# Holding back scatters of routing records at four points of a hybrid S5 and mixture-of-experts step

## What is computed

```python
x = x + ssm_mixer(rmsnorm(x, norm_mix))      # S5 scan, Re(C x) + D u, GELU, then a @ w_out with a gate
x = x + hier_moe(rmsnorm(x, norm_ffn))       # below
y = rmsnorm(x, norm_final)

def hier_moe(x):                             # per token
    g = argmax(softmax(x @ w_rg))            # top 1 of 4 groups
    w1, w2, e1, e2 = top_k(softmax((x @ w_re)[g]), 2)   # top 2 of the 4 experts in it, weights normalised
    return sum over e in (e1, e2) of  p_g * w_e * (silu(x @ w_gate[e]) * (x @ w_up[e])) @ w_down[e]
```

## Time and profile before

| | us |
|---|---|
| median of 3 runs | 830.38 (829.59 to 834.03) |
| profiled execution, own time | 831.41 |
| its span on the core | 829.7 |
| TensorE busy (matmul) | 785.4, 95% |
| VectorE busy | 598.2, 72% |
| ScalarE busy | 412.2, 50% |
| GpSimd busy | 316.4, 38% |
| record scatters L549 | 34 of 1.05 us mean, 324.6 to 436.9 |

### The profile page before, as it was taken

One profiled execution on the slowest core, in us unless ns is written; L12 is line 12 of the kernel. 1 busy time (PEld: TensorE's weight loads), 2 busy tenths in 40 slices (PEclk: granted clock), 3 DMA queues, 4 the chain that ended last, 5 costly groups with the idle time before them and its releaser, 6 DMA issues.

```text
span 829.7 us, 15186 instructions
## 1 busy us (share of the span) xinstructions
PE 785.4 (95%) x4265; PEld 619.3 (75%) x4265; DVE 598.2 (72%) x1143; ACT 412.2 (50%) x770; POOL 316.4 (38%) x416
## 2 busy tenths in 40 slices
PE   6999989999999999998988989999999999999993
PEld 4888866556778778786766868888888888887772
DVE  7998789996534365457776788768687688687843
ACT  7566752225335353342353666647466477466622
POOL 3910011011000002304154566567566766565532
PEclk9999999999999999999999999999999999999997
DMA  8564316897734242323367587557775688786632
GB/s 296 166 224 181 127 29 206 209 156 210 296 118 151 77 153 102 128 108 124 102 230 283 191 304 256 194 190 264 270 252 198 216 287 295 253 301 203 224 116 85
DMA packets 57670, 161.27 MB, mean 194 GB/s; under 512 B 21856, under 2 KB 26464, under 8 KB 50912
## 3 DMA queue, kind: packets, MB, share of 16 engines
q1 hardware_dynamic: 34304, 112.99, 41.6%
q0 software_dynamic: 22976, 47.05, 16.2%
q10 hardware_dynamic: 288, 0.03, 0.0%
HBM read 129.07 MB, written 62.40 MB: 231 GB/s over the span
## 4 chain that ended last, share of the span: by engine, by line
PE 38%; DMA 3%; issue 3%; DVE 2%; POOL 2%; DVEq 1%; ACTq 1%; ACT 1%; POOLq 0%
PE pbig L1391 7%; PE pbig L1395 7%; PE pbig L1392 7%; PE pbig L1410 4%; PE pbig L1412 4%; PE pbig L1411 4%; PE pbig L1327 3%; POOL records L549 1%; DMA xg<-x_mid,recs 1%; PE pbig L1403 1%; DMA WR<-in_w_gu 1%; DMA records<-rec,at_rec 1%; DVE WL L2014 1%; ACT WH L928 1%; DMA low<-records 0%
## 5 line engine op out<-in xcount | busy, mean ns | idle before, releaser
L1391 PE MATMUL pbig<-WH,xgH 128*128 (+1 forms) x304 | 123.9, 408 | 1.2 <-issue 1.1
L1392 PE MATMUL pbig<-WL,xgH 128*128 (+1 forms) x304 | 119.8, 394 | 0.0
L549 POOL DMA_INDIRECT records<-rec,at_rec x34 | 35.6, 1047 | 190.7 <-DVEq L2007 181.3
L1274 PE MATMUL pbig<-w2H,ysH 128*128 128x512 f32 x256 | 105.3, 411 | 0.0
L1275 PE MATMUL pbig<-w2L,ysH 128*128 128x512 f32 x256 | 100.6, 393 | 0.0
L1276 PE MATMUL pbig<-w2H,ysL 128*128 128x512 f32 x256 | 100.5, 393 | 0.0
L2014 DVE SCALAR_TENSOR_TENSOR WL<-WR,gf_p,WH 128x512 f32 (+1 forms) x128 | 86.2, 746 | 0.0
L928 ACT ACTIVATE WH<-WR,gf_p 128x512 f32 (+1 forms) x128 | 80.6, 712 | 3.6 <-DMA WR<-in_w_gu 1.5
L1395 PE MATMUL pbig<-WH,xgL 128*128 (+1 forms) x304 | 77.0, 395 | 0.0
L623 POOL DMA_INDIRECT x_sums<-xg,recs x36 | 61.7, 1713 | 35.7 <-DVE xg L2118 21.8
L946 ACT ACTIVATE sl<-pbig,recs 128x256 f32<-128x256 f32 x40 | 18.9, 473 | 102.8 <-PE pbig L1395 92.8
(11 more groups left out here) (356 smaller groups left out, 1738.3 us busy)
## 6 DMA issues: line engine op xcount, KB each, us to landing
WR<-in_w_gu SPq DMA_DIRECT2D x32, 1024.0 KB
WR<-in_w_dn SPq DMA_DIRECT2D x16, 1024.0 KB
xT<-in_x_cols SPq DMA_DIRECT2D x16, 512.0 KB, 3.7
low<-in_x_rows SPq DMA_DIRECT2D x16, 512.0 KB, 4.6
U<-in_x_rows SPq DMA_DIRECT2D x16, 512.0 KB, 5.1
x_mid<-x SPq DMA_DIRECT2D x16, 512.0 KB, 2.7
x_sums<-x SPq DMA_DIRECT2D x16, 512.0 KB, 4.0
w<-in_w_out SPq DMA_DIRECT2D x1, 4096.0 KB, 13.8
```

What stands on the lines that cost most here:

```text
L1274: pe.matmul(pbig[:, n, :], ysH[b][:, k, :], w2H[n][:, k, :], start=(k == 0), stop=False)
L1391: pe.matmul(pbig[:, 6, :], xgH[b][:, k, :], WH[:, ds(off + k * 2 * DE, 2 * DE)], start=(k == 0), stop=False)
L1392: pe.matmul(pbig[:, 6, :], xgH[b][:, k, :], WL[:, ds(low_ + k * 2 * DE, 2 * DE)], start=False, stop=False)
```

## The change

GpSimd waits at four points inside `file_rows` for a count of `lt_evac`, the semaphore that ScalarE increments when it has copied a tile's logits. The count 11 stands for tile 10, 12 for tile 11, 15 for tile 14, and TT = 17 for tile 16. Each wait stands ahead of one scatter, given by (tile, c). The waits divide the 34 scatters: 4, 4 and 4 of batch 0; 5 and 5 of batch 1; 4 and 4 of batch 2; batch 3 (4) is as before.

```diff
 BATCHES = ((0, 6), (6, 11), (11, 15), (15, TT))
+HOLD = {(2, 0): 11, (4, 0): 12, (8, 1): 15, (13, 0): TT}
 ROUTE_A, POS_AT, ROUTE_B = (7, 11, 15), (8, 12), (9, 13)
...
                 for c in range(2):
+                    if (t, c) in HOLD:
+
+                        pool.wait_ge(S["lt_evac"], HOLD[t, c])
                     pool.indirect_dma_start(tabD, bass.IndirectOffsetOnAxis(ap=at_rec[0:rows, c, t:t + 1], axis=0),
```

## The result

The changed kernel takes 824.38 us (median of 20 runs, 823.09 to 829.53), and the kernel before, run in turn with it, 832.04 us (20 runs, 827.24 to 834.79). The ratio is 0.9924, 95% interval 0.9909 to 0.9939: faster by 0.76%, some 6.3 us, where 4.6 us were forecast (the two medians alone lie 7.66 us apart). The profiled execution takes 825.51 us with a span of 823.8 us, against 831.41 and 829.7 us.

A forecast was written before the change was run, and what follows sets the result against it. TensorE was taken to bound the kernel, losing time to late handshakes beside scatter runs; 1.45, 3.65 and 5.08 us accumulated, limited to 4.6 by gather(3)'s landing: 830.38 - 4.6 = 825.8 us, 8-in-10 range 824.1 to 830.7.

The forecast's parts named there:

- What bounds the stage, and the mechanism: Routing to fourth expert slot: TensorE bounds at 12.94 us per tile; long scatter runs delay signals, above all TensorE to ScalarE.
- three late handshakes: Late ScalarE copies at tiles 10, 14 and 16, inside scatter bursts; losses of 1.45, 3.52 and 1.43 us.
- VectorE as next late: Before tile 15's mixing: first expert's weight cuts limit the gain to 3.65 us, not 4.97; 1.32 us lost.
- Batch 2's hold: Fifth scatter waits for tile 16's copy: costs 0 to 0.2 us; copy 1.43 us less late, 5.08 us gained on TensorE.
- A copy is late beside a group of four: Sign of being wrong: a copy still late although its scatter run is cut to four.
- the records land with the weight loads: Batch 2's last records land when the weight loads drain, 3.65 us earlier, even if the hold costs a microsecond.
- Gather(3): Rows for the fourth expert slot: issued 3.65 us earlier at 438.4, landing 4.6 us earlier at 447.4, where TensorE resumes.
- my rule: Gather(3)'s landing follows the end of the second expert's first loads, not its own issue; 4.6 us earlier, bounds 3.65 and 5.08.
- Gather(0): Behind batch 1's scatters: issued at about 397.1 instead of 394.75, rows wanted at 407.8; covered, barely in the worst case.
- (A): Rival: signals come in time, but gather(3) lands 9.96 us after issue; 826.7 us, variant 828.2; chance 0.20 with variant.
- (B): Rival: something else delays signals, or four or five scatters suffice; delays stay or move; 830.4 us, chance 0.14.
- (C): Rival: holds add to stalls that stay, delaying gather(3) by 1.6 us; 832.0 us, 832.5 with gather(0); chance 0.09.

The follow-up runs named there:

- chip 14: Unedited changed kernel timed again beside the kernel before, on another chip and occasion: 826.03 us against 830.12, ratio 0.9947 (0.9922 to 0.9972).
- split8: Changed kernel with other splits: batch 0 as 8 and 4, batch 1 as 8 and 2, batch 2 as 2 and 6; 827.19 us, one run.
- chip 3: Unedited changed kernel timed a third time beside the kernel before, on another chip: 826.24 us against 825.52, ratio 1.001 (0.9996 to 1.0023).
- hold_batch0: Kernel before plus only the two waits in batch 0: 825.07 us beside 826.35, ratio 0.9987 (0.9965 to 1.001).
- chip 0: Where the kernel before was timed beside itself and beside each batch's hold alone: 826.35 us (35 runs); itself again 827.23, ratio 1.001 (0.999 to 1.003).
- burst22: Changed kernel with its holds replaced by one: batches 0 and 1 in one run of 22 scatters after tile 13's copy; 841.11 us, one run.
- late12: Changed kernel with batch 0's twelve scatters all held until tile 10's logits are copied, other holds unchanged; 830.45 us, one run.

## Why the prediction was right, and where its steps were not

**What bounds the stage, and the mechanism.** Right where the two were first timed. The three late handshakes were the loss, the holds remove the first two entirely, and each gain is there: tile 11's logit matmuls moved by 351.15 - 350.74 - 1.86 = -1.45 us (forecast 1.45), tile 14's by 391.00 - 394.03 - 1.86 = -4.89 us (4.97).

**VectorE as next late.** Right. The mixing of tile 15 starts in the same moment as the weight cut ends, without an idle gap, and moved by 3.72 us (3.65); that of tile 16 by 3.60 us (3.65). Without this step the sum would have had 1.3 us more than the stage could give (4.89 less 3.60).

**Batch 2's hold.** Two sizes were off. Tile 16's copy comes 1.39 us after its matmuls (418.15 - 416.76), so 0.68 of the 1.43 us stayed, with only four scatters ahead of it; chip 14 shows the same, 0.69 us. "A copy is late beside a group of four" was one of the three signs by which I would be wrong, and it came, at less than half the size. The fifth scatter then comes at 419.19. Without the hold it would have come at 419.66 - 3.60 + 1.86 = 417.92, so the hold costs 1.27 us and not 0 to 0.2. Of this, 0.68 is the late copy. The other 0.59 is a price that I had put at nothing: from the end of the awaited copy to the held scatter pass 0.76 us here (418.43 to 419.19), and 0.75 and 0.76 at the two holds of batch 0 (copies end at 339.21 and 352.15), but only 0.28 at batch 1's (391.99 to 392.27). The three stand ahead of a tile's first scatter, the cheap one ahead of its second; the other traces with these holds give the same within 0.02 us. On PE the gain was 4.38 us (ready at 447.93 against 450.45) and not 5.08. That the records land with the weight loads, which was to hide such a delay, held only in part: the loads moved by 3.60 us (415.15 against 416.89), the table load behind the landing by 2.85 us (427.69 against 428.68). It cannot hide the whole 1.27 us.

**Gather(3).** It was issued 2.67 us earlier (forecast 3.65), and the second expert's loads 3.57 us earlier (forecast 4.6). By my rule, landing with the loads, PE's start on its rows should have moved by 3.57 us at most. It moved by 5.72. The first half of the rule holds: the gather's first packets came at 446.93 before and at 445.22 now, moved by 3.57 us, exactly as the loads. In all thirteen traces that show it they come 7.1 to 7.5 us after the issue of the loads. They also come 4.0 to 4.2 us after the gather's own issue in twelve of them (4.9 in the kernel before), so the traces favour the loads, but not by much.

My evidence for the rule was weaker than I took it to be. The 99.9% for the other queue in 443 to 444 says nothing, because a gather moves nothing so soon: gather(2), issued at 430.80 with the engines idle, has its first packet at 432.4, 1.6 us later, and gather(0), issued at 394.75, at 397.05, 2.3 us later. Nor do the engines work for the loads alone until these have drained. In 445 to 446 the kernel before kept them busy for 66.8% with the loads, and the gather still moved nothing. Once its packets were there, in 447 to 448, the two queues took nearly equal numbers of packets (q0 carries the gathers, q1 the loads; packets, MB, share of the 16 engines' time):

```profile
q1 hardware_dynamic: 37, 0.28, 66.5%
q0 software_dynamic: 33, 0.14, 33.7%
```

In the changed kernel the loads fill 444 to 445, and the gathers have 446 to 447 almost to themselves:

```profile
q1 hardware_dynamic: 52, 0.43, 102.6%
```

```profile
q0 software_dynamic: 87, 0.35, 97.2%
q1 hardware_dynamic: 8, 0.02, 6.1%
```

The Trainium skill (DMA: Bandwidth & Descriptors, section Queues, rings and completion order) states an even turn, packet by packet. The 37 and 33 packets agree with that; what held the gather back until 446.93 they do not tell.

What I had taken as fixed was the time from the first packet to the landing. Before, PE waited until 452.04, 5.1 us after it; now it could start 3.0 us after it. Before, gather(4) and gather(5) had been issued (443.71 and 445.16) when service began, now only gather(4) (442.69; the next is at 445.52). That the fewer waiting gathers made the difference is an argument from these times and was not tried. Most other traces fit it (2.8 to 3.1 us where PE waits for the rows), but split8 took 4.2 us with only one gather waiting behind.

**Gather(0).** Wrong, without a cost. I had it at about 397.1, and it was issued at 403.81, 7.2 us later than before (9.06 less 1.86). It waits for the first table load, and I took this to wait for batch 0 alone. It waits for batches 0 and 1: FIRST_TOK is BATCHES[1][1] = 11. In the same way `tab_early` counts the tiles below 15, not below 11. Both are wrong in the description of the kernel ahead of the prediction. SyncE issues that load only at 401.83, 1.2 us after batch 1's last scatter, and its store of tile 15 waits behind it. The profile had shown this: before, the load was issued behind the end of batch 1 (391.58).

```profile
392.74 0.38 SPq L450 DMA_DIRECT2D low<-records  x1
```

Batch 1 also ended later than I had it, since its scatter at 393.63 took 3.22 us, beside VectorE's weight cut (393.73, 2.28 us); whether the cut is the cause was not tried. PE took up the rows at 409.55, so 5.7 us were enough.

**The size.** Forecast 4.6 us of gain and 825.8 us, measured 6.3 us by the ratio and 824.38 us. The stage of the trace gives 5.7: two terms fell short together by 0.7 us on PE, and gather(3)'s landing more than made up for it. That the total came out near the forecast is therefore in part luck. The rest lies between executions. The base of three runs (830.38) was 1.7 us below the median of twenty, and the delays of the kernel before differ from one execution to the next.

**The rivals.** (A) did not come: PE started on gather(3)'s rows 7.0 us after its issue, not 9.96. (B), that something else makes the signals late, is half true: the run of scatters is needed, and so is something outside the program. It also named a move of the delay to another handshake, and a small one came, at tile 15 (below). On the chips without it the outcome is the one that (B) gives, no change. (C) did not come, but its mechanism, a held scatter that delays gather(3), may stand behind PE's wait of 1.12 us on chip 3 and of 2.14 us in split8. It is not shown: hold_batch0, where batch 2 is not held, has such a wait of 0.76 us too, and the kernel before on chip 0 has none.

**Open.** What makes the handshakes late in one place and not in another, and whether it belongs to the chip or to the occasion. The scatters are issued at the same pace in both (1.27 us apart), so the issue times hold no hint. Open also is from which length of run on it matters, and how the gain of the first comparison divides among the holds except as the trace's terms divide it.

## What to carry to other kernels

A wait that nothing on the core explains, beside a run of work on another engine, is worth a cheap pause in that run, placed where the waiting engine has just been served. Before the gain is believed, the kernel should be timed on several chips and occasions: here the same two programs differ by 0.76%, 0.5% and nothing, and a single profile of the kernel before cannot say which it will be. A pause is not free either: here 0.76 us passed from the awaited copy to a held scatter that is a tile's first, and 0.28 us to one that is its second. And when a transfer is issued beside a backlog, its landing cannot be had from its issue time and one duration: here the same gather took 6.9 to 10.0 us from issue to landing.

## What the runs showed of the hardware that I had not expected

- The same twelve scatters in an unbroken run delay a copy by 3.8 us in one place and by nothing on chip 0. The kernel before takes 830 to 832 us or 826 us accordingly.
- Twenty-two scatters in one run delay a copy by 7.2 us, and they reach TensorE itself: between 412 and 416 us of burst22 it shows four gaps of 0.34 to 1.19 us that nothing in the profile ends.
- A late handshake can cost more than its wait. In late12 PE stood idle 2.25 us before its fold matmul, and the granted clock fell to half. From 348.91 the next logit matmuls took 19.79 us to come, 5.9 more than the 13.9 between tiles 11 and 12 elsewhere. The stretch 352 to 360 us of late12 (columns as in the earlier trace rows, granted clock third from the end):

```profile
352.00:360.00 8.00, 5.50 (x19) 4.36 (x19) 3.62 (x10) 3.80 (x9) 1.05 (x2) 0.66 0.17 66
```

In the kernel before, the idle time of 3.38 us at 394.03 left the clock at 2.4 GHz (granted clock 1.00). On chip 14 the same kernel was idle for 3.16 us at the same place (400.26), and the clock in 400 to 406 was 0.50. So the length of the idle time alone did not decide it. The row is the first of the two:

```profile
390.00:395.00 5.00, 1.62 (x21) 0.91 (x20) 5.00 (x7) 1.94 (x4) 1.52 (x3) 1.00 0.04 2
```

- A copy was late beside gathers as well. In the changed kernel gather(0) and gather(1) are issued at 403.81 and 405.30, across tile 15's handshake, and its copy comes 1.18 us after its matmuls, 0.47 us late. On chip 14 it comes 1.15 us after them; on chip 3 it comes after 0.71 us, and in the kernel before too, where gather(1) was issued at 401.44 and the matmuls came at 406.97. TensorE and ScalarE:

```profile
403.94 0.65 PE L1313 MATMUL pbig<-xnT,wr_sb 128*32 128x128 f32 x16
```

```profile
405.12 0.28 ACT L911 ACTIVATE lt<-pbig 128x128 f32<-128x128 f32 x1 [3.13 <-PE pbig L1313]
```
